# Right operands of an output projection made during the retention, and norms by a power on GpSimd

## The reference

```
h = rms_norm(x, g);  z = h @ w_in         # q,k,v,gate of attention; q,k,v,gate of retention; merge gates
attention: 8 q heads, 2 key heads, width 64; q and k normalised by head (rms_norm), rotated
           ya = (silu(ga) * softmax(q k^T / 8) v) @ w_branch_attn
retention: 4 heads, width 128, chunks of 128: a scan forward, a scan backward, summed
           yb = (silu(gr) * group_norm(o)) @ w_branch_ret
x = x + (sigmoid(gA) * ya + sigmoid(gB) * yb) @ w_out
```

## Time and profile before

| | |
|---|---|
| median of 3 runs (lowest, highest) | 1848.42 us (1846.0, 1848.89) |
| profiled execution, its span | 1849.25 us, 1847.4 us |
| mean granted TensorE clock | 0.989 |
| busy: PE, DVE, ACT, POOL | 1755.8, 1264.8, 801.0, 672.2 us |
| DMA traffic | 113.08 MB |

### The profile page before, as it was taken

One profiled execution on the slowest core, in us unless ns is written; L12 is line 12 of the kernel. 1 busy time (PEld: TensorE's weight loads), 2 busy tenths in 40 slices (PEclk: granted clock), 3 DMA queues, 4 the chain that ended last, 5 costly groups with the idle time before them and its releaser, 6 DMA issues.

```text
span 1847.4 us, 30201 instructions
## 1 busy us (share of the span) xinstructions
PE 1755.8 (95%) x10592; PEld 1556.1 (84%) x10592; DVE 1264.8 (68%) x2626; ACT 801.0 (43%) x1791; POOL 672.2 (36%) x581
## 2 busy tenths in 40 slices
PE   6999999999999999998989999999999999999986
PEld 5887878899999888887787888889999998888875
DVE  6789678725543387769986876795345544867798
ACT  4478448722123243334344873683222223433333
POOL 0157227624233323223601771484224322232240
PEclk9999999999999999999999999999999999999998
DMA  7000000011011323224130001001011023222322
GB/s 270 24 12 13 28 23 24 25 46 47 23 34 35 131 70 96 81 93 157 46 118 24 24 1 50 12 13 47 24 46 45 27 88 114 71 78 86 131 80 92
DMA packets 136665, 113.08 MB, mean 61 GB/s; under 512 B 16480, under 2 KB 115040, under 8 KB 136544
## 3 DMA queue, kind: packets, MB, share of 16 engines
q1 hardware_dynamic: 134144, 106.20, 18.0%
q10 hardware_dynamic: 2400, 5.31, 0.8%
HBM read 90.52 MB, written 20.97 MB: 60 GB/s over the span
## 4 chain that ended last, share of the span: by engine, by line
PE 73%; DVE 16%; ACT 4%; issue 4%; DMA 2%; POOL 1%; SPq 0%; DVEq 0%; ACTq 0%; POOLq 0%
PE ps L758 17%; PE ps L760 17%; PE ps L759 17%; PE ps L894 5%; PE ps L883 4%; PE ps L907 3%; PE ps L909 3%; DVE xh L2173 2%; PE ps L1000 2%; DVE pT_lo L1804 2%; PE ps L984 1%; DVE nmx L1796 1%; DVE lsum L2151 1%; DVE us L1905 1%; ACT pp L1289 1%
## 5 line engine op out<-in xcount | busy, mean ns | idle before, releaser
L758 PE MATMUL ps<-w_hi,hT_hi 128*128 128x256 f32 (+1 forms) x1280 | 391.1, 306 | 13.0 <-DVE hT_lo L1669 4.4
L760 PE MATMUL ps<-w_hi,hT_lo 128*128 128x256 f32 (+1 forms) x1280 | 376.5, 294 | 0.0
L759 PE MATMUL ps<-w_lo,hT_hi 128*128 128x256 f32 (+1 forms) x1280 | 376.3, 294 | 0.0
L758 PEld LDWEIGHTS ps<-w_hi,hT_hi 128*128 128x128 f32 x1280 | 244.9, 191 | 17.9 <-DVE hT_lo L1669 6.1
L759 PEld LDWEIGHTS ps<-w_lo,hT_hi 128*128 128x128 f32 x1280 | 245.3, 192 | 0.3
L760 PEld LDWEIGHTS ps<-w_hi,hT_lo 128*128 128x128 f32 x1280 | 244.6, 191 | 0.0
L612 POOL TENSOR_SCALAR pp<-pp,rrc 128x1024 f32<-128x1024 f32 x128 | 144.0, 1125 | 161.0 <-DVE rrc L1809 155.1
L1804 DVE TENSOR_TENSOR pT_lo<-ps,pT_hi 128x512 fp32r<-128x512 f32 x256 | 164.2, 682 | 24.4 <-ACT pT_hi L1300 22.9
L558 POOL TENSOR_SCALAR w_hi<-raw 128x1024 fp32r<-128x1024 f32 x65 | 69.1, 1063 | 286.2 <-PE ps L760 250.0
L894 PE MATMUL ps<-idf,pp 128*128 128x128 f32 x1024 | 141.5, 278 | 18.4 <-DVE pT_lo L1804 12.3
L1796 DVE TENSOR_REDUCE nmx<-ps 128x1 f32<-128x1024 f32 x128 | 154.4, 1206 | 2.6 <-PE ps L883 2.6
(11 more groups left out here) (215 smaller groups left out, 4106.8 us busy)
## 6 DMA issues: line engine op xcount, KB each, us to landing
raw<-w_in SPq DMA_DIRECT2D x167, 256.0 KB, 3.2
xs<-xh SPq DMA_DIRECT2D x2, 4096.0 KB, 16.2
ys<-y_st SPq DMA_DIRECT2D x32, 256.0 KB, 2.1
hb<-ys SPq DMA_DIRECT2D x16, 512.0 KB, 4.4
xh<-xs SPq DMA_DIRECT2D x8, 1024.0 KB, 7.4
raw<-w_a SPq DMA_DIRECT2D x16, 256.0 KB, 3.2
raw<-w_r SPq DMA_DIRECT2D x16, 256.0 KB, 3.3
w<-w_o SPq DMA_DIRECT2D x4, 1024.0 KB, 6.1
```

The source lines that it names most:

```text
L758: nc.tensor.matmul(outp, ah, bh, start=(start and i == 0), stop=False)
L759: nc.tensor.matmul(outp, ah, bl, start=False, stop=False)
L760: last = nc.tensor.matmul(outp, al, bh, start=False, stop=(stop and i == len(pairs) - 1))
```

## The change

It does four things. (1) w_out is loaded in four slices k of 1 MB during the retention, by ScalarE's queue. For each slice and product a step n = 7k + i makes one 128x512 piece of a right operand: GpSimd sums (for the five products that need it), ScalarE rounds, VectorE subtracts, and ScalarE issues a DMA of hi and lo (0.5 MB) to a new DRAM tensor wos. R_AT gives each step a place; place 16h + t is block t of first_pass(h), 16h + 8 + t that of second_pass(h). (2) The output projection loads its right operands from wos by SyncE's queue, four DMAs of 0.5 MB a product; right_sum, right_hi and right_lo of before are gone. (3) The norms of q and k are made block by block on GpSimd, `(ss/64 + eps) ** -0.5` in two operations; VectorE's norms() and rsqrt of q and k are gone, and split, rotate and the turns follow each block by a fixed distance (late = 2 for j = 0, 1 for j = 1). (4) gqk and ctA are loaded by two DMAs, for j = 1 once the last product with the values (pv_done) of j = 0 is done. The hardware loops of the retention are written out.

```diff
+LATE = (2, 1)
+K_R = 4
+R_ORDER = (1, 5, 0, 2, 3, 4, 6)
+N_R = K_R * N_P
+R_PLACES, R_LOAD = (0, 2, 3, 5, 6, 8, 9), 10
+R_AT = {2 + (R_LOAD + 3) * k + o: k * N_P + i for k in range(K_R) for i, o in enumerate(R_PLACES)}
+R_LOADS = {2 + (R_LOAD + 3) * k + R_LOAD: k + 1 for k in range(K_R - 1)}
+            def r_free(eng, L, n):
+                if L * N_R + n >= 2:
+                    eng.wait_ge(r_out[n % 2], 16 * ((L * N_R + n) // 2))
...
@@ SyncE, tables of q and k @@
-                                sp.wait_ge(phase_end, L * PH_L + j * 3)
+                                sp.wait_ge(pv_done, L * (KVH * 2 * T) + j * (2 * T))
+                            sp.dma_start(gqk[:], qkn[bass.ds(L, 1), :].to_broadcast([P, QK_W])).then_inc(b_tab, 16)
+                            sp.dma_start(ctA[:], rope_a).then_inc(b_tab, 16)
...
@@ SyncE, output projection @@
+                def right_in(p, halves=(0, 1)):
+                    for h in halves:
+                        c = right_wide(p, h)
+                        for s, to in enumerate(right_slot(p, h)):
+                            src = wos[p, :, s, 1024 * h:1024 * h + 1024].rearrange("p (b c) -> p b c", c=c)
+                            sp.dma_start(to.bitcast(F32), src).then_inc(o_r[R_SLOT[p]][h], 16)
...
+                for p in range(3, N_P):
+                    if p != 4:
+                        sp.wait_ge(o_done, L * (4 * N_P) + 4 * N_P + 4 * ({3: 0, 5: 1, 6: 2}[p] + 1))
+                    right_in(p)
...
@@ GpSimd, attention @@
+                    for t in range(T):
+                        pool.wait_ge(b_ssum, bt + 1)
+                        nc.gpsimd.tensor_scalar(ss[:, o], ss[:, o], 1.0 / HD, EPS, ALU.mult, ALU.add).then_inc(b_ms, 1)
+                        pool.wait_ge(b_ms, bt + 1)
+                        nc.gpsimd.tensor_tensor(rs[:, o], ss[:, o], minus_half[:], ALU.pow).then_inc(b_rs, 1)
                     pool.wait_ge(b_proj, L * (KVH * T) + j * T + T)
...
@@ GpSimd, retention @@
+                def right_sum(place):
+                    if place + 1 not in R_AT:
+                        return
+                    n = R_AT[place + 1]
+                    blocks = RIGHT[R_ORDER[n % N_P]]
+                    if len(blocks) == 1:
+                        return
+                    pool.wait_ge(r_in, 16 * (L * K_R + n // N_P + 1))
+                    r_free(pool, L, n)
+                    (r, c, q) = blocks
+                    a, b = (wo_raw[:, 2 * x[0] + x[1]] for x in (r, c))
+                    nc.gpsimd.tensor_tensor(r_total(n), a, b, ALU.add if q > 0 else ALU.subtract).then_inc(r_sum, 1)
                 def rotate(h, fills):
                     for t in range(T):
                         pool.wait_ge(c_rot, c0 * 3 + 3 * t + 3)
                         nc.gpsimd.tensor_tensor(ra[:, t], ra[:, t], rb[:, t % 2], ALU.add).then_inc(c_o, 1)
...
+                        right_sum(2 * T * h + t)
-                with pool.Fori(0, RH - 1) as h:
+                for h in range(RH - 1):
                     fill_qk(h)
+                    for t in range(T):
+                        right_sum(2 * T * h + T + t)
                     rotate(h + 1, h)
...
@@ ScalarE, retention @@
+                def right_steps(place):
+                    if place - 1 in R_AT:
+                        n = R_AT[place - 1]
+                        act.wait_ge(r_hi, L * N_R + n + 1)
+                        act.wait_ge(r_lo, L * N_R + n + 1)
+                        a, k = 2 * (n % 2), n // N_P
+                        act.dma_start(wos[R_ORDER[n % N_P], :, :, 512 * k:512 * k + 512],
+                                      quad(ur_lo, 4)[:, a:a + 2].bitcast(F32)).then_inc(r_out[n % 2], 16)
+                    if place in R_LOADS:
+                        right_load(R_LOADS[place])
+                    if place in R_AT:
+                        n = R_AT[place]
+                        i = n % N_P
+                        if len(RIGHT[R_ORDER[i]]) == 1:
+                            act.wait_ge(r_in, 16 * (L * K_R + n // N_P + 1))
+                            r_free(act, L, n)
+                        else:
+                            act.wait_ge(r_sum, (L * K_R + n // N_P) * 5 + i - 1)
+                        nc.scalar.copy(r_rows(n)[0], r_src(n)).then_inc(r_hi, 1)
                 def first_pass(h, done):
                     for t in range(T):
+                        right_steps(2 * T * h + t)
...
+                right_load(0)
                 first_pass(0, None)
...
@@ VectorE, retention @@
+                def right_lo(place):
+                    if place in R_AT:
+                        n = R_AT[place]
+                        dve.wait_ge(r_hi, L * N_R + n + 1)
+                        hi, lo = r_rows(n)
+                        V.tensor_tensor(lo, r_src(n), hi.bitcast(F32), ALU.subtract).then_inc(r_lo, 1)
                 def first_pass(h, done):
                     for t in range(T):
+                        right_lo(2 * T * h + t)
                         if done is not None and 2 <= t <= 3:
                             cross(done, 2 * t - 4)
                             cross(done, 2 * t - 3)
                         rotate(h, t, done)
...
@@ VectorE, attention @@
                         outputs(t)
-                        if t == 2:
-                            norms(0)
...
+                        if t == late:
+                            gain()
+                        if t >= late + 1:
+                            split(t - late - 1)
+                        if t >= late:
+                            rotate(t - late)
```

More of the change, by code:

```diff
@@ L108, with build @@
 IN_W = (0, 1, 3, 5)
-def build(nc, x, gains, w_in, qn, kn, decays, gn_w, w_a, w_r, w_o,
-          ident, rope_a, rope_r, dist, idx, xs, ys, out):
+def build(nc, x, gains, w_in, qkn, decays, gn_w, w_a, w_r, w_o,
+          ident, rope_a, rope_r, dist, idx, xs, ys, wos, out):
     with ExitStack() as ctx:
@@ L168, in build @@
             pT_lo = sb(p2, "pT_lo", [2, T, 256], F32R)
+        with ExitStack() as pz:
+            sb(pz, "below_wo", [2 * SEQ])
+            wo_raw = sb(pz, "wo_raw", [4, 512])
         ur_hi = sb(ctx, "ur_hi", [KA, SEQ], F32R)
@@ L205, in build @@
             w12 = sb(pg, "w12", [4, 512])
+        with ExitStack() as pg:
+            first_r = sb(pg, "first_r", [4, 512], F32R)
         gB = sb(ctx, "gB", [DM])
@@ L856, in turn @@
                         last.then_inc(b_tr, 1)
+                    late = LATE[j]
                     for t in range(T):
@@ L866, in _ @@
                                 turn_x(t + 1)
-                        if t >= 5:
-                            turn(t - 5)
-                    for i in range(5):
+                            if part == 0 and t >= late + 2:
+                                turn(t - late - 2)
+                    for i in range(6):
                         gate(i // 2, i % 2)
-                        turn(i + 3)
-                    gate(2, 1)
+                        if i < late + 2:
+                            turn(T - 2 - late + i)
                     b2 = L * (KVH * T) + j * T
@@ L1142, in last_product @@
                     pe.wait_ge(o_alo, L * (2 * N_P) + 2 * ORDER_A.index(p) + 2)
-                    pe.wait_ge(o_blo, L * (2 * N_P) + 2 * N_P + 2 * p + 2)
+                    for h in range(2):
+                        pe.wait_ge(o_r[R_SLOT[p]][h], 32 * (L * R_USES[R_SLOT[p]] + R_NTH[p] + 1))
                     for i in range(4):
@@ L1399, in second_pass @@
                             update(h, t - 1)
+                right_load(0)
                 first_pass(0, None)
-                with act.Fori(0, RH - 1) as h:
+                for h in range(RH - 1):
                     second_pass(h)
@@ L1549, in _ @@
                 squares(0, 0, 1, 3)
-                right_hi(6)
                 squares(1, 0, 0, 4)
@@ L1973, in second_pass @@
                     for t in range(T):
+                        if h + 1 < RH:
+                            right_lo(2 * T * h + T + t)
                         if t >= 1:
@@ L1984, in _ @@
                 first_pass(0, None)
-                with dve.Fori(0, RH - 1) as h:
+                for h in range(RH - 1):
                     second_pass(h)
@@ L2189, in _ @@
                 merge_a(K - 1, 0)
-                right_lo(0)
                 give(K - 1, 4)
```

254 lines of the change are left out of this document (91 added, 163 removed).

## The result

The changed kernel takes **1893.8 us** (median of 5 runs, 1891.67 to 1897.69) against 1848.89 for the kernel before on the same chip: 1.0239 times as long, 95% interval 1.0227 to 1.0251. Forecast: 1876, range 1843 to 1902. The direction and the range were right; the loss was put at 28 us and is 45. The profiled execution has 1891.95 us around a span of 1890.0.

The account below looks back on a forecast made before the run. TensorE, busy 95%, was taken to bound the kernel, leaving only its idle and slow-clock time to win. Retention +67, norms -21, output projection -15 gave +31; less 3, 1848.4 + 28 = 1876 us, range 1843 to 1902.

Parts of the forecast that it names:

- Retention: Retention of both layers: the added steps' order makes TensorE wait, 33.5 us a layer, +67 us in all.
- The chain that the prediction wrote down: Retention, head 1: rotation, addition, fill, sum, copy, subtraction, cross sums in turn; TensorE idle 3.3 us at its third cross product.
- what place 23 holds back: Retention, head 1: the step at place 23 delays the last rotation and so the first decay_scores(), some 1.8 us.
- Norms of q and k: Projection of q and k: norms leave VectorE; 5 us gained per second key head, 5.5 per first, -21 us in all.
- The waits for L1739 are gone: Sign for the changed trace: TensorE's four waits of about 2.8 us for split() disappear.
- The first key head of layer 0: Projection of q and k: of 6.8 us idle and 1.7 of slow clock, 3 left standing, 5.5 us gained.
- Output projection: Right operands come by DMA, unloading VectorE: 8 us a layer and 1 at the end, less late loads; -15 us together.
- rival (c): Retention chain holds and output projection loads are late too, 15 to 25 us a layer more: 1900 to 1925; chance 0.09.
- The 3 us taken off: Whole kernel: 3 us off the +31 total, since part of the slow clock stretches falls into waits anyway.
- (a): Retention: sums reach ScalarE before VectorE needs them, steps hidden, 0 to 10 us a layer: 1812 to 1832; chance 0.14.
- (b): Retention: half of the chain counts, 17 to 24 us a layer: 1846 to 1858; chance 0.12.
- (d): Second key heads: slow GpSimd norms, 5 us a power, delay rotations, +10 us a key head: about 1900; chance 0.03.

Follow-up runs that it names:

- run 1: Changed kernel with VectorE's low half of a right operand issued behind its tile's cross sums and rotation, likewise in second passes: 1847.13 us, ratio 0.9990.
- run 2: Changed kernel with GpSimd's sum for the next place issued ahead of its wait for this tile's rotation: 1856.25 us, ratio 1.0033.
- run 3: Changed kernel with the edits of run 1 and run 2 together: 1844.06 us, ratio 0.9977 to the kernel before.
- run 4: Changed kernel with the turn of q and k behind both halves of a tile's projection in second key heads: 1891.79 us, ratio 1.0244.
- run 6: Run 4 with the last turns at later gate halves and VectorE's first gate ahead of its last rotation: 1878.18 us, ratio 1.0155.
- run 7: Kernel before with only the norms half of the change and run 6's later turns, right operands as before: 1830.61 us, ratio 0.9892.
- run 9: Changed kernel with edits of run 3 and run 6, a buffer for the sums, early first load, 28 places set one by one: 1815.06 us, ratio 0.9814.
- run 11: Run 9 without GpSimd's 20 sums a layer, so five of seven right operands are not the product's: 1805.41 us, ratio 0.9760.
- run 10: Run 9 with places 18, 19 and 34 moved to 19, 21 and 35, so no sum runs beside the backward pass: 1817.31 us, ratio 0.9822.

## Why the prediction was right, and where it was not

**Retention: right in mechanism and nearly in size.** +72.4 us against +67. The chain that the prediction wrote down, step by step, is the one in the timeline, 2.94 us of wait for 3.3 forecast, and runs 1 to 3 show that the order makes it: the same work in another order costs 12 us a layer instead of 36, and 4.3 with chosen places, the sums' own buffer and the early load. By head in layer 0, from one head's first scores to the next: head 0 +6.0 (forecast 9.7), head 1 +10.0 (9.2), head 2 +13.6 (8.9), head 3 +6.2 (5.7). Cut there, head 0's slow clock falls to head 1, and what place 23 holds back (1.8 forecast for head 1) falls to head 2, where TensorE waits 0.64 and 1.60 us behind it; so the forecasts compare as 8.0, 9.1, 10.7 and 5.7. The first load, issued at 371.5 us behind the mask as foreseen, had landed at 376.2, 4.7 us for 6.5; these 1.8 us are about what head 0 costs less than its 8.0. Head 2 was underrated: TensorE waits for the backward pass (1.50 us, 0.62 before), for cross() (2.94) and for the last rotation that it needs (1.87), each of the latter two with a slow clock behind; the prediction counted neither the first of them nor the second slow clock. The clock of 0.50 for 3.4 us stood behind the waits as forecast.

**Norms of q and k: wrong.** The step that failed: "So the second key head gives back its 4.0 us of idleness and the 1.7 us of slow clock but for 0.7: 5 us." It was +2.3 and +1.2 us. The work did leave VectorE (33.9 us busy in 60, 40.8 in 65 before), but TensorE's wait there was never for VectorE's busy time; it was for a split placed late in VectorE's order, and the new order has its own: five waits of 0.5 us, since turn(t - 3) stands in front of the second half of a projection and its split behind VectorE's outputs of the block before, and 2.5 us with the slow clock at the end, since the last turn now stands behind the third half gate, where it had stood behind the fifth. The prediction took the wait at L1739 as gone with the norms and didn't lay the new order against TensorE's, as it had done for the retention. Runs 4, 6 and 7 show it: with the last turns where their splits end, the second key heads are 3.2 to 4.3 us shorter than before, near the 5 foreseen. So one of its signs failed too: "The waits for L1739 are gone"; they are 15.1 us.

The first key head of layer 0 came out at -5.2 us for -5.5, but not as reckoned, and that is luck: two slow stretches of 3.4 us each went there (at 44 and 78 us before, 3.3 us of work together) where one was counted, and only some 2 us of idle time; a wait of 2.26 us for the split stays. With 13.5 us the second key heads are most of the 17.8 us by which the forecast missed.

**Output projection: right, and too small.** Layer 0's stretch, the next first key head included, gave 15.3 us for 12.5 forecast (11.1 of them in the projection itself, put at 7: its products take 89.3 us before and 78.1 now), layer 1's 12.6 for 8 (8.9 in the products, and 3.7 in VectorE's tail at the very end, put at 1). These 7.4 us beyond the forecast hide part of what the norms and the retention cost more. TensorE is busy 78.0 of 78.0 us there: the whole of 8.5 us idle and the slow clock went, not all but 2.3, so what I let stand ("less the 1.3 of the turn", "less 1 that stays"), the 1 us for late loads and the 1 us of the tail were the terms mis-sized. Products wait for no load, at 223 GB/s and with 9.8 us for one of 512 KB, three times a store's 3.1: rival (c) is out. VectorE's 63.2 us busy in 78 answers to the 60 forecast.

**The 3 us taken off** for slow stretches that fall into waits: some did fall there (3.5 us of head 0's 6.8 in layer 0), but there were more of them than the four a layer counted. Each layer's retention has 20.5 us of slow clock, and what TensorE worked in it costs 8 us a layer against the 6.8 counted. The rest, some 3 us, lies outside the stages: the median is 3.8 us above the profiled span now and was 1.0 before.

**Rivals.** (a), hidden steps, is refuted for this order, and is nearly what runs 9 and 11 show for another. (b) asked for half the chain; all of it counted (its own upper end adds up to 1860, not 1858). (d) doesn't bind: the power on GpSimd takes 1.41 us, above the 1 us taken and at the upper bound of 1.4, and the rotations wait for it once, 0.2 us. Rows of GpSimd in the changed kernel:

```profile
L710 POOL TENSOR_TENSOR w1x<-wo_raw 128x512 f32<-128x512 f32 x40 | 51.4, 1284 | 51.1 <-DMA wos<-ur_lo 51.1
L647 POOL TENSOR_TENSOR rs<-ss,minus_half 128x5 f32<-128x5 f32 x32 | 45.2, 1413 | 2.7
```

## What to carry to other kernels

Spare busy time on an engine says that work fits, not that it is free; what it costs is set by where it stands in that engine's order. Write down, for each step put in, what it waits for and what is queued behind it, and put it behind the work that the bottleneck waits for and its producer ahead of the producer's own waits: here two moved calls were worth 50 us (run 3). When work is taken off an engine, lay the new order against the consumer's as well; here the wait fell only when the turn was moved to where its split ends (15.6 us in run 6, and as much in run 7).

## What the runs showed of the hardware that I had not expected

A power on GpSimd takes 1.41 us for 5 values a partition (row above), about as long as its sum of 512 (1.28), while its scaling of the same 5 values takes 0.38: in the second key head GpSimd's busy time rose from 7.8 us to 20.2, and VectorE waited for it 0.2 us in the whole kernel.

That GpSimd holds VectorE up was in the prediction as a bound; that it makes about half of what is left (1.8 of 3.9 us a layer, runs 9 to 11) was not expected. The backward pass's 48 operations have a mean of 573 ns where no sum runs beside them (run 10) and 648 ns in run 9, where those of heads 0 and 1 have one (the two rows in turn are run 9's and run 10's):

```profile
L1934 DVE SCALAR_TENSOR_TENSOR us<-us,dcur 128x128 f32<-128x128 f32 x48 | 31.1, 648 | 6.3 <-ACT us L1420 4.9
```

```profile
L1934 DVE SCALAR_TENSOR_TENSOR us<-us,dcur 128x128 f32<-128x128 f32 x48 | 27.5, 573 | 6.3 <-ACT us L1420 4.9
```

The Trainium skill ("SBUF — State Buffer", SBUF: two separate sides) says that GpSimd and a VectorE operation with two SBUF inputs share ports by an exclusive lock: the one that starts first holds them for the whole instruction and the other blocks. The backward pass's operation has two such inputs (both from us), and the traces agree. The fourth of the six takes 1.25 us beside the sum of 1.30 in run 9 and 0.35 with no sum in run 10, and the whole pass 4.20 and 3.30: the 0.9 us between them is that one operation. The third takes 1.01 us beside the fill of 1.09, in both.
